# Column sums of x1's squares in four 32-column groups, root and reciprocal on 144 columns, and six weight rests moved from GpSimd to VectorE

## The reference

```
x1 = x + gate * rms_norm(conv_out, g_post)            # residual after layer 0
ckv, kpe = split(rms_norm(x1, g_in) @ w_down, [512, 64])
h1 = rms_norm(x1, g_pre) * (1 + scale) + shift        # input of layer 1
qa, z = split(h1 @ w_in, [512, 2048])
rms_norm(x, g) = x * rsqrt(mean(x*x over the 2048 features) + 1e-6) * g
```

## Time and profile before

| | |
|---|---|
| median of 3 runs | 2122.98 us |
| lowest and highest | 2120.01 and 2124.22 us |
| span of the profiled execution, first to last instruction | 2121.4 us |
| TensorE busy | 2013.0 us, 95% of the span |
| VectorE, ScalarE, GpSimd busy | 1317.6, 811.2 and 253.9 us |
| mean granted TensorE clock | 0.978 of full speed |

### The profile page before, as it was taken

The page is one execution under the profiler, slowest core; times in us unless marked ns, Lnnn a source line. Parts: engine busy times, 40 slices in busy tenths (PEclk is TensorE's granted clock), DMA queues, the critical chain, the costliest instruction groups (busy, mean ns, idle before and its releaser), DMA issues. The chain is left out here.

```text
span 2121.4 us, 42392 instructions
## 1 busy us (share of the span) xinstructions
PE 2013.0 (95%) x16248; PEld 1886.6 (89%) x16248; DVE 1317.6 (62%) x1961; ACT 811.2 (38%) x1228; POOL 253.9 (12%) x166
## 2 busy tenths in 40 slices
PE   6789999999999999999979999999999989989994
PEld 4589999999999999999979999999888866679994
DVE  2687777777777777897769620223443445658776
ACT  3143333333333333454445532223453434434542
POOL 0100000000000000000004334333122121200001
PEclk9899999999999999999989999999999999999997
DMA  9955555555566555734463222234212358742456
GB/s 358 399 201 187 191 200 204 205 200 184 207 210 202 194 204 188 283 105 143 152 251 148 92 70 90 100 123 161 89 49 90 99 176 281 236 162 81 142 161 203
DMA packets 129379, 372.31 MB, mean 175 GB/s; under 512 B 13378, under 2 KB 40898, under 8 KB 126978
## 3 DMA queue, kind: packets, MB, share of 16 engines
q1 hardware_dynamic: 123010, 351.81, 48.1%
q0 software_dynamic: 6272, 19.14, 3.2%
HBM read 343.11 MB, written 27.79 MB: 175 GB/s over the span
## 5 line engine op out<-in xcount | busy, mean ns | idle before, releaser
L686 POOL TENSOR_TENSOR w_lo<-w_raw,w_hi 128x1024 fp32r<-128x1024 f32 (+1 forms) x89 | 212.1, 2384 | 1553.0 <-ACT w_hi L1312 1553.0
L1368 ACT ACTIVATE w_hi<-w_raw 128x1024 fp32r<-128x1024 f32 x180 | 190.6, 1059 | 339.3 <-PE ps L808 185.5
L1851 DVE TENSOR_TENSOR w_lo<-w_raw,w_hi 128x1024 fp32r<-128x1024 f32 x186 | 227.8, 1225 | 126.2 <-ACT w_hi L1368 118.6
L804 PE MATMUL ps<-operand_hi,w_hi 128*128 128x288 f32 x1080 | 290.0, 295 | 0.0
L804 PE MATMUL ps<-operand_lo,w_hi 128*128 128x288 f32 x1080 | 289.7, 294 | 0.0
L804 PE MATMUL ps<-t_hi,w_hi 128*128 128x288 f32 x992 | 271.6, 300 | 4.9 <-DVE c_v L1993 2.8
L804 PE MATMUL ps<-t_lo,w_hi 128*128 128x288 f32 x992 | 266.6, 295 | 0.0
L1312 ACT ACTIVATE w_hi<-w_raw 128x1024 fp32r<-128x1024 f32 (+1 forms) x91 | 92.8, 1019 | 289.8 <-PE ps L745 186.3
L804 PEld LDWEIGHTS ps<-operand_hi,w_hi 128*128 128x128 f32 x1080 | 202.8, 188 | 0.1
L804 PEld LDWEIGHTS ps<-operand_lo,w_hi 128*128 128x128 f32 x1080 | 202.7, 188 | 0.0
L804 PEld LDWEIGHTS ps<-t_hi,w_hi 128*128 128x128 f32 x992 | 186.3, 188 | 14.5 <-issue 11.2
(11 more groups left out here) (353 smaller groups left out, 4022.4 us busy)
## 6 DMA issues: line engine op xcount, KB each, us to landing
w_raw<-wstream SPq DMA_DIRECT2D x177, 512.0 KB, 3.4
ada_ring<-adastream SPq DMA_DIRECT2D x114, 512.0 KB, 4.7
a<-wstream SPq DMA_DIRECT2D x90, 512.0 KB, 4.6
s<-wstream SPq DMA_DIRECT2D x45, 512.0 KB, 3.3
ada_first_ring<-adastream SPq DMA_DIRECT2D x36, 512.0 KB, 9.8
ada_third<-adastream SPq DMA_DIRECT2D x32, 512.0 KB, 6.5
x_residual<-x_in SPq DMA_DIRECT2D x8, 1152.0 KB, 9.8
tiles<-y_park SPq DMA_DIRECT2D x8, 1152.0 KB, 8.9
```

The lines of the kernel that those rows point to most:

```text
L686: pool.tensor_tensor(WL[:, n.slot, 0:width], WR[:, n.slot, 0:width], WH[:, n.slot, 0:width].bitcast(F32), ALU.subtract).then_inc(w_lo_read ...
L804: pe.matmul(PS[:, bank, 0:HALF], WH[:, c.slot, k * P:(k + 1) * P], x(k), start=(first and k == 0 and x is hi), stop=False, skip_group_chec ...
L1368: act.activation(WH[:, c.slot, :], raw, ACT.Copy).then_inc(w_hi_ready, 1)
L1851: dve.tensor_tensor(WL[:, c.slot, :], raw, WH[:, c.slot, :].bitcast(F32), ALU.subtract).then_inc(w_lo_ready, 1)
```

## The change

Four things are edited.

1. **Squares.** `add_two_squares` takes the place of `add_squares` in the x1 stage. It runs at odd k only, between the hi products of k - 1 and those of k, and sums the squares of both tiles. For each it takes four products with a 128 x 32 matrix of ones, one for each quarter of the tokens (144 columns), into the partitions 32g to 32g + 31 of bank 6. The first use of `add_squares`, at the kernel's start, is as before.
2. **Root and reciprocal** run on the tile `rstd_quarters` (RQ, 128 x 144), in which each 32 partitions hold one quarter of the tokens. Then TensorE spreads them (`spread_quarters`): four float32 products of a broadcast identity column with RQ, into columns 288 to 431 of banks 0 to 3. They are put between chunk 8 and chunk 9. ScalarE copies them into R0 (128 x 576).
3. **Weight rests** of chunks 2 to 7 are formed by VectorE, in `residual` at t = 4, 6, ... 14, between `operand_lo` of tile t - 1 and the add of tile t. GpSimd begins with chunk 8.
4. **Semaphore counts.** `cols_made` is counted once more, so the values waited for at its second use change.

```diff
--- before.py
+++ after.py
@@ -59,6 +59,7 @@
 RG = 32
 ADA0 = 2 * KT // AT4
 HG = 4
+QUAD = T // 4
 
 
 W_THREE = KT // 2
@@ -219,6 +220,7 @@
         UP = at("u_prompt", uo, [P, TP + 2])
         US = at("u_sample", uo + TP + 8, [P, NB, NS + 2])
         R1 = at("rstd1", uo, [P, T])
+        RQ = at("rstd_quarters", uo, [P, QUAD])
         WK.append(at("wk3", mo, [P, CT * P]))
         to = place(3 * T)
         HI_AT = (xo + 4612 + 5 * PGT, xo + 4612 + 5 * PGT + R, xo + 4096, po + 11648, po + 13568, mo,
@@ -312,6 +314,10 @@
 
         def part_block(t, kh, a, lo=0, n=HK):
             return t[:, :].rearrange("p (k a n) -> p k a n", a=2, n=HALF)[:, HK * kh + lo:HK * kh + lo + n, a, :]
+
+        def rstd_turn(use):
+
+            return 2 * use - 1
 
         def rope_chunk(g):
 
@@ -689,11 +695,11 @@
             with pool.Fori(0, W_PRE // 2) as i:
                 rest(Chunk(0, 2, i), CH2)
                 rest(Chunk(1, 2, i), CH2)
-            pool.wait_ge(w_lo_ready, W_KV + 2)
-            assert (W_PAIR2 - W_KV) % 2
-            with pool.Fori(0, (W_PAIR2 - W_KV) // 2 - 2) as i:
-                rest(Chunk(W_KV + 2, 2, i))
-                rest(Chunk(W_KV + 3, 2, i))
+            pool.wait_ge(w_lo_ready, W_KV + W_THREE)
+            assert (W_PAIR2 - W_KV) % 2 and W_THREE % 2 == 0
+            with pool.Fori(0, (W_PAIR2 - W_KV - W_THREE) // 2 - 1) as i:
+                rest(Chunk(W_KV + W_THREE, 2, i))
+                rest(Chunk(W_KV + W_THREE + 1, 2, i))
             rest(Chunk(W_OUT + 1))
 
             def load_latents(b, odd, used=None):
@@ -720,12 +726,14 @@
 
         @block.tensor
         def _(pe):
-            def tile(n, p, ready=None, each=None, hi=OH, lo=OL, kts=KT, cols=P, split=2):
+            def tile(n, p, ready=None, each=None, hi=OH, lo=OL, kts=KT, cols=P, split=2, between=None):
 
                 per = kts // split
                 last = None
                 for q in range(split):
                     c = n + q
+                    if q and between:
+                        between()
                     pe.wait_ge(w_hi_ready, c.at(1))
                     for kk in range(per):
                         k = q * per + kk
@@ -883,7 +891,7 @@
                         pe.wait_ge(added[1], n + 1 + BEGUN)
                     last = pe.matmul(PS[:, 6, b:b + 1], ACC[:, o:o + P], small("ones", 0, 1), start=True, stop=True)
                 last.then_inc(cols_made, 1)
-                pe.wait_ge(col_rstd, use)
+                pe.wait_ge(col_rstd, rstd_turn(use))
                 for b, o in enumerate(TOKENS):
                     a, o = b // 3, o - b // 3 * HALF
                     last = pe.transpose(PS[:, 6 + a, o:o + P], RC[:, 8 + b:9 + b].broadcast_to([P, P]), ident)
@@ -896,6 +904,24 @@
                     last = pe.matmul(PS[:, 6 + a, 0:HALF], small("ones"), TT[k % 2][:, a * HALF:(a + 1) * HALF],
                                      start=(k == 0), stop=(k == n - 1), skip_group_check=True)
                 last.then_inc(used[k % 2] if k < n - 1 else stat_done, 1)
+
+            def add_two_squares(k):
+
+                for j in (k - 1, k):
+                    pe.wait_ge(xsq_ready[j % 2], KT // 2 + j // 2 + 1)
+                    for g in range(4):
+                        last = pe.matmul(PS[32 * g:32 * g + 32, 6, 0:QUAD], small("ones", 0, 32),
+                                         TT[j % 2][:, g * QUAD:(g + 1) * QUAD],
+                                         start=(j == 0), stop=(j == KT - 1), skip_group_check=True)
+                    last.then_inc(xsq_used[j % 2] if j < KT - 1 else stat_done, 1)
+
+            def spread_quarters():
+
+                pe.wait_ge(col_rstd, 2)
+                for g in range(4):
+                    last = pe.matmul(PS[:, g, HALF:HALF + QUAD], ident[:, 32 * g:32 * g + 1].broadcast_to([P, P]), RQ[:, :],
+                                     start=True, stop=True)
+                last.then_inc(cols_made, 1)
 
             pe.sem_inc(pv_done, BEGUN)
 
@@ -1004,9 +1030,9 @@
             for j in range(2):
                 pe.wait_ge(co["evac"][j], KT // 2 + BEGUN)
             for i in range(W_THREE):
-                three_tiles(Chunk(W_KV + i), i, xg_ready, each=lambda k: add_squares(xsq_ready, xsq_used, k, KT, KT // 2))
+                three_tiles(Chunk(W_KV + i), i, xg_ready, each=lambda k: add_two_squares(k) if k % 2 else None)
             pe.wait_ge(var_ready, 2)
-            tile(Chunk(W_KV + W_THREE), 3)
+            tile(Chunk(W_KV + W_THREE), 3, between=spread_quarters)
             pe.wait_ge(kv_evac, 3)
             n = Chunk(W_KV + W_THREE + 2)
             pe.wait_ge(w_hi_ready, n.at(1))
@@ -1312,7 +1338,7 @@
                 act.activation(WH[:, n.slot, 0:width], WR[:, n.slot, 0:width], ACT.Copy).then_inc(w_hi_ready, 1)
 
             def column_root(use):
-                act.wait_ge(cols_made, 2 * use - 1)
+                act.wait_ge(cols_made, 3 * use - 2)
                 act.activation(RC[:, 0:6], PS[:, 6, 0:6], ACT.Sqrt, bias=RC[:, 6:7], scale=1.0 / D).then_inc(col_roots, 1)
 
             def root(k, reg):
@@ -1547,7 +1573,10 @@
                 act.activation(TT[k % 2][:, :], X[:, k * T:(k + 1) * T], ACT.Square).then_inc(xsq_ready[k % 2], 1)
                 if k % 2 and k >= 3:
                     round_w(Chunk(W_KV + k // 2 + 1))
-            root(2, 3)
+            act.wait_ge(var_ready, 2)
+            act.activation(RQ[:, :], RQ[:, :], ACT.Sqrt).then_inc(root_ready, 1)
+            act.wait_ge(cols_made, 3)
+            act.activation(R0[:, :].rearrange("p (g n) -> p g n", g=4), PS[:, 0:4, HALF:HALF + QUAD], ACT.Copy).then_inc(rstd_out, 1)
 
             def h1_prompt(q):
 
@@ -1776,7 +1805,7 @@
 
                 dve.wait_ge(col_roots, use)
                 dve.reciprocal(RC[:, 8:14], RC[:, 0:6]).then_inc(col_rstd, 1)
-                dve.wait_ge(cols_made, 2 * use)
+                dve.wait_ge(cols_made, 3 * use - 1)
 
             def mod_turn(n, bank):
 
@@ -2178,6 +2207,8 @@
                     c = slice(t * T, (t + 1) * T)
                     dve.tensor_tensor(halves(B1[:, c]), halves(B1[:, c]), r if t else PS[:, 6:8, 0:HALF], ALU.mult).then_inc(normed, 1)
                     rest_xg(t)
+                    if t >= 4 and t % 2 == 0:
+                        part_lo(Chunk(W_KV + t // 2), WR[:, (W_KV + t // 2) % 2, :])
                     dve.wait_ge(normed, t + 1)
                     dve.tensor_tensor(X[:, c], X[:, c], B1[:, c], ALU.add).then_inc(x1_ready, 1)
 
@@ -2196,7 +2227,11 @@
             rest_xg(KT)
             scale_table(48 + KT, ("gpre", KT), 1.0)
             step(dve.memset(ACC[:, :], 0.0))
-            rstd(2, D, 3)
+            dve.wait_ge(stat_done, 2)
+            dve.tensor_scalar(RQ[:, :], PS[:, 6, 0:QUAD], 1.0 / D, EPS, ALU.mult, ALU.add).then_inc(var_ready, 1)
+            dve.wait_ge(root_ready, 2)
+            dve.reciprocal(RQ[:, :], RQ[:, :]).then_inc(col_rstd, 1)
+            dve.wait_ge(rstd_out, 2)
 
             def latent(t):
                 dve.tensor_tensor(halves(CKV[:, t * T:(t + 1) * T]), pair(t), halves(R0[:, :]), ALU.mult).then_inc(kv_evac, 1)
```

## The result

| | before | changed |
|---|---|---|
| median of 17 runs each | 2122.47 us | 2128.14 us |
| span of the profiled execution | 2121.4 us | 2126.5 us |

What follows compares the result with a forecast made beforehand. Bound: the gate at chunk 12's first product, where TensorE waits for ScalarE, whose work hangs on R0. It comes 5.8 us later: 2121.4 + 5.8 = 2127.2, with the median 1.6 above the span 2128.8 us; range 2124.5 to 2132.5.

Steps and rivals of the forecast that it cites:

- Bound by the gate: Chunk 12's first product, waiting for ScalarE, through which the rest passes: forecast at 1189.6 instead of 1183.76, 5.8 us later.
- Squares 0.29 us a tile: TensorE's squares in the x1 stage: 0.29 us a tile instead of 0.98, 11 us less work over the stage.
- The spread 0.98 and handing over 0.2: Between chunks 8 and 9: TensorE's four spread products take 0.98 us, then 0.2 us until ScalarE's copy.
- VectorE's pair of 6.58 us: VectorE's x1 loop: a pair of tiles takes 6.58 us, including a 0.78 us stall for ScalarE's rounding.
- R0 5.3 us later: The reciprocal root, behind chunk 8 and the spread: there at 1158.7 instead of first used at 1153.44.
- Wait before chunk 9: TensorE stands still 1.9 us before chunk 9, whose rounding is held up by ScalarE's copy into R0.
- Exclusion of VectorE and GpSimd up to prompt(1): VectorE's h1(0) and h1(1) and GpSimd's rests of chunks 9 and 10 add up: done at 1170.4.
- The clock: Rival: TensorE's gaps bring a slow clock at chunk 9 or in the last pair, 3.2 us more, 2132.0 us; 14%.
- TensorE's saving comes through: Rival: x1 loop falls to TensorE's 5.3 us a pair, 0.6 to 4.4 us faster, 2119 at best; 6%.
- up to 10: Gain in us from five shorter pairs, earlier first squares and less meeting with GpSimd, set against the 5.8 us loss.
- the exclusion isn't there: Rival: VectorE and GpSimd don't exclude each other in h1, 2.2 us late, 2125.2 us; 18%.
- ScalarE catches up: Rival: ScalarE catches up or the stall before chunk 9 hides, gains of 2 to 3 us, 2126 us; 12%.

Runs made afterwards that it cites:

- e5: The changed kernel with VectorE's weight rest put behind the add of the even tile instead of ahead of it: 2122.46 us, 0.9997 of the kernel before.
- e1: The changed kernel with TensorE's spread moved from between chunks 8 and 9 to before chunk 8: 2121.95 us, 0.9999 of the kernel before.
- e3: The changed kernel with ScalarE's rounding of chunk 9 put ahead of its wait for the spread and the copy: 2126.45 us, 1.0015 of the kernel before.
- e7: The changed kernel with GpSimd forming only 8 of 1024 columns of the rests of chunks 9 to 11, result incomplete: 2125.57 us, 1.0011 of the kernel before.
- e6: The changed kernel with the weight rest behind the add and the spread before chunk 8: 2117.26 us, 0.9977 of the kernel before.
- e2: The changed kernel with the weight rests of chunks 2 to 7 given back to GpSimd: 2127.43 us, 1.0021 of the kernel before.
- e4: The kernel before with only the weight rests of chunks 2 to 7 moved to VectorE, ahead of the even tiles' adds: 2123.20 us, 1.0002 of the kernel before.
- e8: The kernel of e4 run once more, unedited: 2125.62 us in a single run.

## Why the prediction was right

- **Bound by the gate, not by TensorE's work: right.** TensorE was busy 5.8 us less in the stage's window and the kernel got slower. The tail behind chunk 12 is the same to 0.2 us.
- **Squares 0.29 us a tile: measured 0.43, the term that was mis-sized.** By the count that gave 0.98 before, a pair costs TensorE 5.61 us and not 5.3, and the stage saves 8.7 us and not 11. The forecast took the time of the groups alone and not what they cost the products beside them. It did no harm, since VectorE set the pace; had TensorE set it, the time would have been off by some 2 us (an estimate: 0.3 us a pair over 7 to 8 pairs).
- **The spread 0.98 and handing over 0.2: right.** ScalarE's copy began 1157.99 - 1156.81 = 1.18 us after the spread did.
- **VectorE's pair of 6.58 us: measured 6.60**, the stall 0.70 instead of 0.78. Chunk 8 began at 1150.42 (forecast 1150.5). e5 shows the cause: with the add first the stall is gone and the pair takes 5.66.
- **R0 5.3 us later: measured 5.27** from the first add. e1 shows that the place of the spread makes it late, and e1 and e3 together that this decides: e3 takes only the wait before chunk 9 away and keeps 3.24 us of the loss.
- **Wait before chunk 9: forecast 1.9, measured 1.68.** e3 adds what the forecast only used in passing: the late rounding of chunk 9 also puts GpSimd's rest in VectorE's way, so that undoing it gives 2.1 us.
- **Exclusion of VectorE and GpSimd up to prompt(1):** forecast 1170.4, measured 1169.97. The forecast counted 3.8 us for the two rests in the way; they cost (3.80 - 2.55) + (2.49 - 0.43) = 3.3. Together with 0.4 us assumed for h1(2), where ScalarE waited 0.24, that makes chunk 12 come at 1189.09 instead of 1189.6. e7 measures the whole exclusion at 3.0 us at the gate.
- **The clock.** A rival rested on the Trainium skill, page "TensorE: Matmul & The Clock Gate", section "HAM oscillation — how this bites in real kernels", by which waits between groups of matmuls can throttle the array again and again. The window after the gap of 3.45 us shows a lower mean clock, the later ones full speed:

```profile
1111.80:1116.00 4.20, 4.20 (x31) 3.40 (x32) 3.32 (x5) 2.30 (x3) 0.00 (x0) 0.61 0.04 15
1127.00:1150.00 23.00, 20.65 (x193) 18.47 (x186) 18.23 (x25) 12.11 (x17) 2.29 (x1) 1.00 0.21 69
1150.00:1180.00 30.00, 27.49 (x205) 26.77 (x203) 21.05 (x16) 16.22 (x23) 10.88 (x4) 1.00 0.58 228
```

A mean of 0.61 lies between the levels of 1.2 and 2.4 GHz, so part of it ran at the lower one. It cost nothing at the end: TensorE used up its spare time in the next pair and waited again from 1124.98 on. In e5, where the gap at this place is 2.87 us, the 4.2 us behind it show a clock of 1.00. The gaps of 0.8 us in the later pairs and the 1.68 us before chunk 9 left it at full speed. So the trace agrees with the rule for the long gap and shows nothing of it for the short ones, and the rival's case, a slow stretch in the last pair or at chunk 9, did not come.
- **The rivals.** That TensorE's saving comes through is what e6 does, and by the condition named, a shorter VectorE pair; the pair needed was not under 5.4 us, since 5.66 with an early spread is enough. (The prediction's "up to 10" less 5.8 is 4.2 us, not 4.4.) That the exclusion isn't there is refuted by e7. That ScalarE catches up did not happen: from prompt(1) to the rounding of chunk 12 it took 18.03 us, 17.67 before.

## What to carry to other kernels

Before an engine's work is made cheaper, look for the engine with the next slower pace in the same loop; here it stood 0.15 us a pair behind, and of 8.7 us of saved work 0.6 was left at chunk 8. A new dependent step (a spread, a broadcast) belongs where its input is ready, not behind the next long block of an in-order queue, and what it makes wait on another engine should not stand ahead of work that is ready. And where an instruction waits for another engine's late result, put first what feeds that engine.

## What the runs showed of the hardware

- VectorE instructions with both inputs in SBUF and GpSimd's reading take turns whole, whichever came first: GpSimd's 8 columns took 2.58 us behind h1(2), and 0.21 while VectorE scaled the latents, one of whose inputs is in PSUM (e7). In the changed kernel h1(0) took 3.80 us, not 2.55, behind a rest that GpSimd had begun 1.02 us before it.
- Sums of squares in four 32-column groups with 144 moving float32 columns each cost 0.43 us for all 576 tokens, and 0.98 before as two products of 288 columns over the full array, both from the length of a pair of tiles without waits (5.61 and 6.70 us). By the start of the next product alone it is 0.31 and 0.76. No run separates the price of the groups from that of interrupting the products once a pair instead of twice.
- In the profiled executions the stage's first add came between 1091.66 and 1097.86 us (the latter in e2, the others up to 1093.94), which is more than the whole effect. The intervals of the timed runs are about 0.1% wide to either side, so 0.2% is told from nothing only just. The one kernel with two traces (e4 and e8) gave 91.90 and 91.78 us from the first add to chunk 12; how far other distances repeat was not measured.
